# Three of four feed-forward tiles turned by VectorE and a trip through device memory, instead of by TensorE

## What is computed

```python
def squared_relu_mlp(h, w1, w2):
    z = jax.nn.relu(h @ w1)
    return (z * z) @ w2

for i in range(DEPTH):                      # DEPTH = 2
    ...                                     # attention, pooling, projections
    x = x + squared_relu_mlp(rms_norm(x, ffn_norm[i]), w_ff1[i], w_ff2[i])
```

## Time and profile before

| | us |
|---|---|
| median of three runs | 3082.58 |
| the profiled execution | 3082.89 |
| its span | 3081.1 |
| PE busy | 3024.2 (98%) |
| PEld busy | 2503.5 (81%) |
| DVE busy | 1760.4 (57%) |
| ACT busy | 1498.4 (49%) |
| POOL busy | 51.0 (2%) |
| device-memory traffic over the span | 186 GB/s |

### The profile page before, as it was taken

How to read it: one execution, slowest core, us unless ns; L and a number is a source line. 1 busy time by engine, 2 the same in 40 slices (tenths; PEclk the granted TensorE clock), 3 DMA queues, 4 the chain that set the end, 5 groups by cost and what they waited for, 6 DMA issues and landing times.

```text
span 3081.1 us, 37226 instructions
## 1 busy us (share of the span) xinstructions
PE 3024.2 (98%) x13900; PEld 2503.5 (81%) x13900; DVE 1760.4 (57%) x2334; ACT 1498.4 (49%) x2019; POOL 51.0 (2%) x81
## 2 busy tenths in 40 slices
PE   8999999999999999999999999999999999999998
PEld 6877888888888778778888888888888888787886
DVE  6536554545455676865554545455556557786554
ACT  6534434434344565654434444344444547786333
POOL 0000000000000000000000000000000000010000
PEclk9999999999999999999999999999999999999999
DMA  7545565565655555545565665655775555665664
GB/s 255 183 129 173 191 198 184 191 190 187 194 178 185 170 165 158 165 147 188 191 196 186 192 185 190 189 175 199 217 206 180 154 174 166 197 209 198 225 239 151
DMA packets 301161, 573.80 MB, mean 186 GB/s; under 512 B 18640, under 2 KB 43600, under 8 KB 300240
## 3 DMA queue, kind: packets, MB, share of 16 engines
q1 hardware_dynamic: 293248, 541.13, 55.8%
q0 software_dynamic: 7184, 29.63, 2.8%
q10 hardware_dynamic: 576, 0.94, 0.1%
HBM read 561.15 MB, written 10.49 MB: 186 GB/s over the span
## 4 chain that ended last, share of the span: by engine, by line
PE 85%; DVE 7%; ACT 5%; issue 2%; DMA 1%; DVEq 0%; ACTq 0%
PE acc L1683 26%; PE acc L1685 26%; PE acc L1684 26%; PE tp L1701 2%; DVE wlo L1180 2%; ACT whi L876 1%; DVE wlo L1175 1%; PE sd L1764 1%; PE sd L1746 1%; ACT prob L1093 1%; PE sd L1852 1%; ACT qk L1101 0%; ACT whi L879 0%; ACT L1093 0%; DVE set_lo L1279 0%
## 5 line engine op out<-in xcount | busy, mean ns | idle before, releaser
L1683 PE MATMUL acc<-whi,set_hi 128*128 128x512 f32 x4096 | 1620.2, 396 | 25.0 <-DVE wlo L1180 15.8
L1685 PE MATMUL acc<-whi,set_lo 128*128 128x512 f32 x4096 | 1597.3, 390 | 0.0
L1684 PE MATMUL acc<-wlo,set_hi 128*128 128x512 f32 x4096 | 1596.7, 390 | 0.0
L1180 DVE TENSOR_TENSOR wlo<-raw,whi 128x1024 fp32r<-128x1024 f32 x944 | 1130.4, 1222 | 592.6 <-ACT whi L876 591.7
L876 ACT ACTIVATE whi<-raw 128x1024 fp32r<-128x1024 f32 x944 | 969.9, 1057 | 642.1 <-PE acc L1685 611.7
L1683 PEld LDWEIGHTS acc<-whi,set_hi 128*128 128x128 f32 x4096 | 770.4, 188 | 197.7 <-DVE wlo L1180 25.8
L1685 PEld LDWEIGHTS acc<-whi,set_lo 128*128 128x128 f32 x4096 | 770.1, 188 | 162.8
L1684 PEld LDWEIGHTS acc<-wlo,set_hi 128*128 128x128 f32 x4096 | 770.8, 188 | 154.2
L1275 DVE TENSOR_TENSOR set_lo<-tp,set_hi 128x1024 fp32r<-128x1024 f32 x40 | 49.0, 1225 | 197.3 <-ACT set_hi L992 197.3
L992 ACT ACTIVATE set_hi<-tp 128x1024 fp32r<-128x1024 f32 x40 | 41.1, 1026 | 209.4 <-PE tp L1701 209.4
L1175 DVE SCALAR_TENSOR_TENSOR wlo<-raw,par,whi 128x512 fp32r<-128x512 f32 x160 | 111.9, 748 | 53.0 <-ACT whi L879 52.2
(11 more groups left out here) (229 smaller groups left out, 1167.0 us busy)
## 6 DMA issues: line engine op xcount, KB each, us to landing
raw<-in_w_ff SPq DMA_DIRECT2D x512, 512.0 KB, 4.5
raw<-in_w_in SPq DMA_DIRECT2D x248, 512.0 KB, 4.3
raw<-in_w_out SPq DMA_DIRECT2D x96, 512.0 KB, 4.4
raw<-in_w_mem_kv SPq DMA_DIRECT2D x32, 512.0 KB, 4.7
raw<-in_w_proj_a SPq DMA_DIRECT2D x32, 512.0 KB, 4.2
raw<-in_w_proj_b SPq DMA_DIRECT2D x32, 512.0 KB, 5.4
raw<-in_w_kv SPq DMA_DIRECT2D x48, 256.0 KB, 3.3
raw<-in_w_in SPq DMA_DIRECT2D x48, 256.0 KB, 3.7
```

The lines of the kernel that those rows point to most:

```text
L1180: V.tensor_tensor(wlo[:, c], raw[:, c], whi[:, c].bitcast(f32), ALU.subtract).then_inc(w_lo, 1)
L1683: T.matmul(o, h[:, tok], whi[:, c], start=first, stop=False)
L1684: T.matmul(o, h[:, tok], wlo[:, c], start=False, stop=False)
L1685: ins = T.matmul(o, l[:, tok], whi[:, c], start=False, stop=last)
```

## The change

Of the four tiles of a chunk, the first three are no longer transposed by PE. DVE transposes the blocks of 32x32 inside `stage_b` with two instructions (`turn`, at slab 1 right behind the squaring) and writes them to `blocks`, the first quarter of `u`. POOL waits for that, stores `blocks` (512 KB) to device memory, waits until it has landed, and reads it back with four transfers of 128 KB, each onto 32 partitions of `turned`, the second quarter of `u`. ACT and DVE then make `set_hi` and `set_lo` from `turned` instead of `tp`; this is at slab 1 of the group after, ahead of the next `epi_relu2`, instead of at slab 5. The fourth tile of each chunk goes by PE as before. The first `w_ff2` group now waits for two tiles at slab 0, for the third at slab 4, for the fourth at slab 6. Turned tiles are 3 x 8 = 24.

```diff
+    def turned(self, slab_turn, slab_split, source, dst, kt, gain=None):
+        t, n = self.tails, self.turns
+        self.tails += 1
+        self.turns += 1
+        self.at("dve", slab_turn, "turn", t, source)
+        self.at("pool", slab_turn, "shuffle", t, n)
+        self.at("act", slab_split, "tail", t, dst, kt, gain, ("turned", n))
+        self.at("dve", slab_split, "tail", t, dst, kt, gain, ("turned", n))
...
-            sc.tail(S * (g + 1) + 3, S * (g + 1) + 5, ("staged", sc.staged), z, 4 * i)
+            if i < 3:
+                sc.turned(S * (g + 1) + 1, S * (g + 2) + 1, ("staged", sc.staged), z, 4 * i)
+            else:
+                sc.tail(S * (g + 1) + 3, S * (g + 1) + 5, ("staged", sc.staged), z, 4 * i)
...
+        blocks, turned = u[:, 0:TB * GW], u[:, TB * GW:2 * TB * GW]
...
+            def shuffle(t, n):
+                pool.wait_ge(sm["tail_tp"], at(t + 1))
+                dma(turn_dram, blocks).then_inc(sm["bounced"], 16)
+                pool.wait_ge(sm["bounced"], at((n + 1) * 16))
+                for d in range(4):
+                    dma(turned[32 * d:32 * (d + 1), :].rearrange("i (q c) -> i q c", q=4),
+                        turn_dram[:, 256 * d:256 * (d + 1)].rearrange("(q i) c -> i q c", q=4))\
+                        .then_inc(sm["shuffled"], 16)
...
             def tail(t, dst, kt, gain, lent=None):          # ACT
-                act.wait_ge(sm["tail_tp"], at(t + 1))
+                if isinstance(lent, tuple):
+                    act.wait_ge(sm["shuffled"], at((lent[1] + 1) * 64))
+                else:
+                    act.wait_ge(sm["tail_tp"], at(t + 1))
...
+            def turn(t, source):                            # DVE
+                source_ready(dve, source)
+                for b in range(TB):
+                    o = blocks.rearrange("p (d m b t) -> p b m d t", d=4, m=4, b=TB)[:, b]
+                    ins = V.transpose(o, stage_b[:, GW * b:GW * (b + 1)].rearrange("p (m d t) -> p m d t", m=4, d=4))
+                ins.then_inc(sm["tail_tp"], 1)
...
                                 # PE, in the loop
-                                if k == 3 and s in (0, S - 2):
-                                    pe.wait_ge(sm["tail_lo"], at(cc * 4 + (info["tail0"] + (3 if s == 0 else 4))))
+                                if k == 3 and s in (0, S - 4, S - 2):
+                                    ready = info["tail0"] + {0: 2, S - 4: 3, S - 2: 4}[s]
+                                    pe.wait_ge(sm["tail_lo"], at(cc * 4 + ready))
...
-                                if s == 3 and k < 4:
+                                if s == 3 and k == 3:
```

More of the change, by code:

```diff
@@ L1 @@
+import itertools
 import math
@@ L111, in __init__ @@
         self.tails = 0
+        self.turns = 0
         self.staged = 0
@@ L298, in ffn @@
             if i == 0:
-                sc.groups[g].need[0] = [("tail_lo", sc.tails - 1)]
-                sc.groups[g].need[S - 2] = [("tail_lo", sc.tails)]
+                for k, left in ((0, 2), (S - 4, 1), (S - 2, 0)):
+                    sc.groups[g].need[k] = [("tail_lo", sc.tails - left)]
             sc.epilogue(g, "add", GW * i)
@@ L556, in tail_bank @@
         def tail_bank(lent):
+            if isinstance(lent, tuple):
+                return turned.rearrange("p (q n t) -> p n q t", q=4, t=32)
             if lent == "sd":
@@ L848, in x_back @@
                 dma(gpost, A["post"]).then_inc(sm["post_in"], 16)
-            steps = dict(pool_w=pool_w, mem_again=mem_again, x_spill=x_spill, gate_store=gate_store,
+            def shuffle(t, n):
[6 more added lines that the diff above has]
+                        .then_inc(sm["shuffled"], 16)
+            steps = dict(shuffle=shuffle, pool_w=pool_w, mem_again=mem_again, x_spill=x_spill, gate_store=gate_store,
                          gate_load=gate_load, merge_store=merge_store, merge_load=merge_load, lru_w=lru_w,
                          x_back=x_back)
-            for s in sorted(sc.steps["pool"]):
-                for name, args in sc.steps["pool"][s]:
-                    steps[name](*args)
+            slabs = sorted(sc.steps["pool"])
+            for g, info in list(sc.loops.items()) + [(GALL + 1, None)]:
+                while slabs and slabs[0] < S * g:
+                    for name, args in sc.steps["pool"][slabs.pop(0)]:
+                        steps[name](*args)
+                if info:
+                    for c, k in itertools.product(range(NCHUNK - 1), range(3)):
+                        shuffle(4 * c + info["tail0"] + k, 3 * c + info["turn0"] + k)
         @block.scalar
@@ L990, in tail @@
                     ins = A_(gt[:, TOK * kt:TOK * (kt + 2)], tp[:, 0:2 * TOK], ACT.Copy)
+                elif isinstance(lent, tuple):
+                    o = sets[dst][0][:, TOK * kt:TOK * (kt + 4)]
+                    ins = A_(o.rearrange("p (n q t) -> p n q t", q=4, t=32), tp, ACT.Copy)
                 elif gain is None:
@@ L1272, in tail @@
                 h, l = sets[dst]
-                if gain is None:
+                if isinstance(lent, tuple):
+                    c = slice(TOK * kt, TOK * (kt + 4))
+                    o, i = (w[:, c].rearrange("p (n q t) -> p n q t", q=4, t=32) for w in (l, h))
+                    ins = V.tensor_tensor(o, tp, i.bitcast(f32), ALU.subtract)
+                elif gain is None:
                     c = slice(TOK * kt, TOK * (kt + 4))
@@ L1642, in _ @@
                                 t = cc * 4 + (info["tail0"] + k)
+                                if s == 1 and 1 <= k < 4:
+                                    tail(cc * 4 + (info["tail0"] + k - 1), info["z"], 4 * (k - 1), None, ("turned", None))
                                 if s == 1 and k < 4:
                                     epi_relu2(cc * 8 + (g + k - 1), info["rst"], q, t)
-                                if s == 5 and k < 4:
+                                if s == 1 and k < 3:
+                                    turn(t, ("staged", q))
+                                if s == 5 and k == 3:
                                     tail(t, info["z"], 4 * k, None)
```

15 lines of the change are left out of this document (11 added, 4 removed).

## The result

| | before | changed |
|---|---|---|
| median of the runs, us | 3082.4 (3081.89 to 3083.31, 4 runs) | 3059.59 (3057.53 to 3060.2, 4 runs) |
| profiled execution, us (span) | 3082.89 (3081.1) | 3059.31 (3057.5) |

The ratio is 0.9924 [0.9912, 0.9937]: faster by 22.8 us. The forecast was 3062.2, its own range 3059 to 3066; the time lies 2.6 us under the forecast, inside the range. The profiled execution lies 3.2 us under the 3062.5 that the forecast's sum gave for it.

A forecast was written before the change was run, and what follows sets the result against it. PE, never idle in the feed-forward parts, was taken as the bound. 3082.9 - 21.6 (transposes removed) + 1.2 (stall at slab 2) = 3062.5, median 0.3 lower: 3062.2 us; own range 3059 to 3066, 8 in 10 within 3059 to 3077.

The forecast's parts named there:

- PE bounds the stage and gives back every instruction: Feed-forward parts: PE is never idle, so removing 24 tiles' transposes gives back 21.6 us, none hidden before.
- The price of a tile: PE time of one tile's eight transposes: 0.91 us by pace, 0.87 on PE itself, taken as 0.90.
- T: Length of one 128x512 block transpose on DVE, taken as 0.685 us from a float32 row of that size.
- The insertion: DVE time added between squaring and slab 2's `wlo`: 2T - 0.06, taken as 1.31 us against 1.32 of slack.
- A: Block transposes on DVE run at about two cycles an element: stall 25.7 us, 3086.7 us in all; chance 0.11.
- C: Block transposes on DVE somewhat slower, T 0.8 to 1.0: stall 5 to 15 us, 3066 to 3076; chance 0.09.
- D: Faster block transposes on DVE, T of 0.425, no stall: 3061.0 us; chance 0.73 together with the forecast.
- The stall at the edge: PE waiting at slab 2 because the added DVE work fills the slack: 0.05 us in 24 places, 1.2 us.
- The split at slab 1 costs nothing: `set_hi` (1.03 us) and `set_lo` (1.23) ahead of `stage_a` fit idle times of 4.38 on ACT, 4.42 on DVE.
- The trip is hidden: Store and four reads through device memory take about 12.1 us, 15.0 by the slowest rows, and cost nothing.
- The window: Time from the end of the block transposes until `set_hi` must start in the next group: 16.9 us.
- Weight loads: Loads of weight slabs, landing in 4.5 us, may take 8.6 beside the trip's added 1 MB per group; still about fit.

The follow-up runs named there:

- one_block: Changed kernel without the store and reads, and one 128x32 block transpose instead of two 128x512 (results not the kernel's): 3057.35 us.
- turn_later: Changed kernel with the two block transposes behind slab 2's `wlo` instead of ahead of it: 3057.43 us.
- trip_plus1: Changed kernel with the store to device memory done twice, the second after the first has landed: 3133.12 us.
- trip_plus2: Changed kernel with the store to device memory done three times, each after the other has landed: 3215.0 us.
- no_trip: Changed kernel without the store and the four reads, splitting the block-transposed tile as it lies (results not the kernel's): 3059.3 us.
- traffic2: Changed kernel with two more 512 KB copies between device-memory tensors in each trip: 3058.07 us.
- again: The changed kernel once more, unchanged: 3057.9 us, 0.9921 of the kernel before.
- x_split3: Changed kernel with ten more tiles, of `x`, turned behind slab 2's `wlo` and split at slab 3, three more semaphore waits: 3052.77 us.

## Where the prediction held, and which step of its sum failed

The mechanism held. What failed is a step of the sum: it starts from one execution of the kernel before, 3082.9, and puts everything outside the 24 places at nothing, because the change touches only the feed-forward parts; that the rest takes the same time in every execution was taken for granted. For the profiled execution the sum gives 3062.5, and 3059.31 was measured. By the table above the missing 3.2 us are: 1.5 at the start, ahead of anything changed; 0.5 in the second part, the gap of before at 1804.15; 0.4 between and behind the parts; and 0.8 in the 24 places themselves, which gave 2 x 10.59 = 21.2 where the sum had 21.6 - 1.2 = 20.4. So three quarters of the miss lie outside the changed places, and the rest is mostly the stall of 1.2 us, which is 0.7.

- *PE bounds the stage and gives back every instruction.* Right. The price of a tile was taken at 0.90 us; 22.67 - 21.76 = 0.91 is what went (one_block), 24 x 0.91 = 21.8 against 21.6.
- *T.* Taken 0.685, measured 0.691 (668 to 714 ns). The insertion was 1.35 instead of 1.31. Rivals A and C fall, and D too (T = 0.425 was not it). One ground given against A was not sound: DVE's scan of 128x256 (L1534) takes 0.692 us in the trace of before, about as long as the other float32 forms take for twice the elements. The block transposes themselves settle it: 0.21 us for 32 elements (one_block) and 0.691 for 512, so (691 - 210) / 480 = 1.00 ns for each further element. The Trainium skill ("Vector Engine (DVE) Microarchitecture Reference", section "The reshape front-end and per-opcode configuration") has one element per cycle per lane; the trace agrees (1.00 ns, against 1 / 0.96 = 1.04 ns for a cycle of the forecast's 0.96 GHz), and 0.691 lies between the row's 0.685 and the forecast's estimate of 0.72 from that page.
- *The stall at the edge.* Taken 0.05 in each place, measured 0.03: 0.7 us instead of 1.2. With 0.2 from the price this makes 0.7 us of the 2.6 by the medians.
- *The split at slab 1 costs nothing.* Right, with less room than said: `stage_a` finds 1.71 us idle before it, `set_hi` none.
- *The trip is hidden.* Right in outcome and wrong in its terms: the store took 3.3 us (not 5.5), since it leaves in a quiet moment, each further issue 0.55 (not 0.71), and the last read 8.4 (not 4.3), with the DMA engines at 1.02 to 1.04 from 320 to 332 us in the changed kernel's profile. The sum is 13.7 instead of 12.1. The rows used were of other moments, and the two large errors cancel in part; that the store found a quiet moment is luck, as turn_later shows with 6.2 us for it and 15.2 for the trip. The window was 16.6 instead of 16.9, so 2.9 us were left in the median and 1.4 in the slowest trip, and 24 us per us of lateness held (trip_plus1, trip_plus2).
- *Weight loads.* Right that they fit; ACT's waits for them rose to 201 us, which the forecast had not said, and cost nothing (no_trip, traffic2).
- *The own range* gave 3.2 us downwards, which just held the first median (3059.59) and not that of `again` (3057.9). Single executions differ by 3.4 us at the start (310.56 to 313.95) and by 3.4 between the parts (529.82 to 533.25), half of the one and all of the other by the number of stretches at half clock; a low end near 3056 was needed. That the first median fell inside is partly luck. The profiles of before and of the changed kernel have the same number of these stretches, so they explain none of the 3.2 us above. How much of the medians' difference they make stays open: of the other executions only the mean clock is on record. In the executions timed beside `again` it is 0.997 or 0.998 for all five of the changed kernel and 0.996 for four of nine of the kernel before, which leaves room for one stretch more, 1.7 us, in some of them.

## What to carry to other kernels

Where one engine has no gap, price its instructions by the pace of the loop with and without them, and look for the one place where the work put in their stead stands ahead of what that engine waits for: here 0.03 us a place, and 0.6 for each further 128x512 transpose. Here a round trip through device memory of half a megabyte (13.7 us) costs nothing, because a window of 16.6 us is free in the loop; once it isn't, each microsecond of lateness is paid in each of the 24 places. Measure such a window by making the trip longer. Before asking where 2 us come from, compare two profiles stretch by stretch, count the stretches at half clock in each, and take a second profile of the kernel before: one execution of it isn't a constant to subtract from. What is taken off the bound engine pays only where the replacement is not queued ahead of the next stage's input: the same ten tiles gave nothing or 5 us according to the slab at which they were split.

## What was not expected of the hardware

- The landing of a store of 512 KB from SBUF depends on the moment: 3.3 us (3.2 to 3.5) in a gap of the other queue, 6.2 when issued some microseconds later (turn_later), 7.4 with the DMA engines at 0.96 to 1.03 (trip_plus1). The fourth read of 128 KB to 32 partitions took 8.4 us (7.3 to 10.0) beside SP's loads, and 3.9 (2.8 to 6.4) where two more stores had moved it to another moment (trip_plus2).
- A megabyte more per trip, copied from one device-memory tensor to another (traffic2), moved neither the loads' effect on PE nor the time.
- The granted clock fell to 0.50 for 3.41 us behind waits of PE of only 2.2 to 2.6 us, in some executions of a program and not in others, at 1.7 us each.
- Gaps of PE without a releaser, 0.3 to 1.4 us, stand at the turns of the hardware loop or just behind them: one or both in each profile of before, none in those of the changed kernel, and more of them again in x_split3.
